# Turning and splitting q and k in the projection stage instead of in attention

## What is computed

```
proj = rmsnorm(x) @ w_in                     # q, k, v (1024 wide each), f, z, xBC, dt, gates
q = rmsnorm(q per head of 64, q_norm_w)      # 16 heads
k = rmsnorm(k per head of 64, k_norm_w)      # is also an output (k_prompt, k_sample)
c = cumsum(log_sigmoid(f + b_f))
s = (q @ k.T) * 64**-0.5 + c[t] - c[s]       # causal; running rows see 256 cached keys too
att = softmax(s) @ v
```

## Time and profile before

| what | value |
|---|---|
| time, median of 3 runs | 2890.07 us (2890.05 to 2894.38) |
| the profiled execution, its own time | 2885.89 us |
| its span, first to last instruction | 2884.1 us |
| mean granted clock of TensorE | 0.978 |
| PE / PEld / DVE / ACT / POOL busy | 95% / 92% / 55% / 35% / 14% |
| DMA queue q1, share of 16 engines | 32.9% |

### The profile page before, as it was taken

One profiled execution on the slowest core, in us unless ns is written; L12 is line 12 of the kernel. 1 busy time (PEld: TensorE's weight loads), 2 busy tenths in 40 slices (PEclk: granted clock), 3 DMA queues, 4 the chain that ended last, 5 costly groups with the idle time before them and its releaser, 6 DMA issues. The chain is left out here.

```text
span 2884.1 us, 47789 instructions
## 1 busy us (share of the span) xinstructions
PE 2737.1 (95%) x18754; PEld 2658.0 (92%) x18754; DVE 1577.2 (55%) x2867; ACT 1022.4 (35%) x2353; POOL 405.7 (14%) x475
## 2 busy tenths in 40 slices
PE   6998979999999999997999989998989999999999
PEld 5997978989999889887999979998989999999999
DVE  4336337656566565565898864464373444434434
ACT  4223336556666655653434331121231111111110
POOL 0000012212122222222555520000000000000000
PEclk8999999999999999998999999999989999999999
DMA  3222232132232222215888873343221111111112
GB/s 115 90 90 53 79 90 91 43 101 76 67 108 76 66 93 58 84 63 140 205 194 214 201 203 121 112 134 128 65 99 58 45 44 45 44 45 44 48 67 96
DMA packets 334448, 273.31 MB, mean 95 GB/s; under 512 B 95952, under 2 KB 311632, under 8 KB 334096
## 3 DMA queue, kind: packets, MB, share of 16 engines
q1 hardware_dynamic: 334224, 270.25, 32.9%
HBM read 197.90 MB, written 72.28 MB: 94 GB/s over the span
## 5 line engine op out<-in xcount | busy, mean ns | idle before, releaser
L411 PE MATMUL banks<-w_hi,xn_hi 128*128 128x256 f32 x1440 | 407.8, 287 | 8.7 <-DVEq L368 5.0
L411 PE MATMUL banks<-w_lo,xn_hi 128*128 128x256 f32 x1440 | 405.5, 286 | 0.0
L414 PE MATMUL banks<-xn_hi,w_hi 128*128 128x352 f32 x1152 | 379.5, 329 | 0.7 <-ACT att_xs L986 0.7
L414 PE MATMUL banks<-xn_hi,w_lo 128*128 128x352 f32 x1152 | 378.7, 329 | 0.0
L414 PE MATMUL banks<-xn_lo,w_hi 128*128 128x352 f32 x1152 | 378.2, 328 | 0.0
L411 PE MATMUL banks<-w_hi,xn_lo 128*128 128x256 f32 x1280 | 366.3, 286 | 0.0
L411 PEld LDWEIGHTS banks<-w_hi,xn_hi 128*128 128x128 f32 x1440 | 276.7, 192 | 10.6 <-DVEq L368 5.1
L411 PEld LDWEIGHTS banks<-w_lo,xn_hi 128*128 128x128 f32 x1440 | 276.6, 192 | 0.2
L1704 PE MATMUL banks<-h_hi,w_hi 128*128 128x352 f32 x768 | 248.8, 324 | 1.9 <-DVEq L1625 1.9
L1704 PE MATMUL banks<-h_lo,w_hi 128*128 128x352 f32 x768 | 248.6, 324 | 0.0
L1704 PE MATMUL banks<-mlp_uhi,w_hi 128*128 128x352 f32 x768 | 248.6, 324 | 0.0
(11 more groups left out here) (293 smaller groups left out, 6160.8 us busy)
## 6 DMA issues: line engine op xcount, KB each, us to landing
w_raw<-in_w_in SPq DMA_DIRECT2D x44, 1024.0 KB, 5.5
scratch_xbc<-att_co SPq DMA_DIRECT2D x32, 512.0 KB, 2.6
ssd_ab<-scratch_acum SPq DMA_DIRECT2D x64, 256.0 KB, 6.0
br_g<-scratch_gates SPq DMA_DIRECT2D x72, 176.0 KB, 2.8
scratch_gates<-hand_tanh SPq DMA_DIRECT2D x48, 176.0 KB, 5.4
scratch_z<-att_z_stage SPq DMA_DIRECT2D x64, 128.0 KB, 1.9
ssd_xbc<-scratch_xbc SPq DMA_DIRECT2D x64, 128.0 KB, 3.4
ssd_xbc<-scratch_xbc SPq DMA_DIRECT2D x128, 64.0 KB, 3.7
```

What stands on the lines that cost most here:

```text
L411: ins = self.nc.tensor.matmul(self.bank(n, P, PW), x[:, k, t * P:(t + 1) * P], w[:, k, :], start=first, stop=end)
L414: ins = self.nc.tensor.matmul(self.bank(n, P, TT), w[:, k, m * P:(m + 1) * P], x[:, k, r * TT:(r + 1) * TT], start=first, stop=end)
```

## The change

The preparation moves from attention to `HeadNormTm`. After a q or k panel is normalized, PE turns it there in blocks of 128 x 128, that is two heads at once, into bank 4; ACT writes the high half (for q with the norm weight and the factor 1/8 as a scale per row), DVE the low half, and SP stores both to two new scratch tensors `q_ops` and `k_ops` [16 heads, 64 + 64 + 4 rows, keys]. There are five groups a panel, one a slot, in slots end + 4 to end + 8, and four groups of cached keys in slots 0 to 3 of the first round. The large reduction is cut into one per tile, in the tile's slot, and the square buffer holds one tile. The weight pass is left for k only. In attention `prep`, `make_hi`, `make_lo` and `double` go; `load_ops` loads each pair as it stands with two DMAs (for keys the first one reads the high rows twice). The freed bank 4 becomes a third bank of the streamed tiles. The bias rows are stored into the same tensors by `Decays`.

```diff
 class HeadNormTm:
+    GROUPS = 5
+    CACHED = 4
+    B_TURNED = 4
...
+    def groups(self, i, n):
+        out = []
+        if i == 0 and 0 <= n < self.CACHED:
+            out.append((n, None))
+        for g in range(self.GROUPS):
+            for k in self.ended(n - 4 - g):
+                out.append((self.CACHED + (i * self.per + k) * self.GROUPS + g, (k, g)))
+        return out
...
     def act(self, act, i, n):
...
             s.nc.scalar.activation(self.stage[x][0:m, t, :], s.bank(n, m, PW), ACT.Copy).then_inc(self.copied, 1)
-            s.nc.scalar.activation(self.sq[0:m, t, :], s.bank(n, m, PW), ACT.Square).then_inc(s.free, 1)
+            if u:
+                act.wait_ge(self.summed, u)
+            s.nc.scalar.activation(self.sq[0:m, :], s.bank(n, m, PW), ACT.Square).then_inc(s.free, 1)
+        for c, src in self.groups(i, n - 1):
+            w = self.width(src)
+            act.wait_ge(self.turned, c + 1)
+            if c >= 2:
+                act.wait_ge(self.ops_stored[c % 2], self.landed(c - 2))
+            s.nc.scalar.activation(self.t_hi[c % 2][:, 0:w], s.core.banks[:, self.B_TURNED, 0:w], ACT.Copy,
+                                   scale=self.scale(src)).then_inc(self.hi_made, 1)
...
     def dve(self, dve, i, n):
...
+        for k, t in s.mine(self, n):
...
+            s.wait_free(dve, i, n)
+            v.tensor_reduce(self.ss[k % 2][0:m, t * self.HEADS:(t + 1) * self.HEADS], self.sq[0:m, :].rearrange("p (h d) -> p h d", d=HD),
+                            AX.X, ALU.add).then_inc(self.summed, 1)
+        for c, src in self.groups(i, n - 1):
+            w = self.width(src)
+            dve.wait_ge(self.hi_made, c + 1)
+            bank, hi, lo = s.core.banks[:, self.B_TURNED, 0:w], self.t_hi[c % 2][:, 0:w].bitcast(F32), self.t_lo[c % 2][:, 0:w]
+            v.scalar_tensor_tensor(out=lo, in0=bank, scalar=self.scale(src), in1=hi, op0=ALU.mult, op1=ALU.subtract).then_inc(self.lo_made, 1)
...
+    def pe(self, pe, i, n):
+        s = self.stream
+        for c, src in self.groups(i, n):
+            if src is None:
+                pe.wait_ge(self.cached, 16)
+            elif src[1] == 0:
+                self.wait_normed(pe, i, src[0])
+            if c:
+                pe.wait_ge(self.lo_made, c)
+            for rows, m, col in self.blocks(c, src):
+                ins = s.nc.tensor.transpose(s.core.banks[:, self.B_TURNED, col:col + m], rows, s.core.ident[0:m, 0:m])
+            ins.then_inc(self.turned, 1)
...
     def sp(self, sp, i, n):
...
+        for c, src in self.groups(i, n - 1):
+            sp.wait_ge(self.lo_made, c + 1)
+            for head, x, cols, col in self.places(i, c, src):
...
+                for part, buf in zip(at, (self.t_hi, self.t_lo)):
+                    sp.dma_start(self.ops[x][head:head + 2, part:part + HD, cols], buf[c % 2][:, col:col + w].bitcast(F32)).then_inc(self.ops_stored[c % 2], 16)
...
 def project_qkv
...
                 for n in range(stream.slots):
                     stream.pe(pe, i, n)
+                    norm.pe(pe, i, n)
...
 def attention_z_xbc
...
-    B_SCORES, B_TURNED, B_PREP, B_OUT, B_TILES = 0, 2, 4, 5, (6, 7)
+    B_SCORES, B_TURNED, B_OUT, B_TILES = 0, 2, 5, (4, 6, 7)
...
-                sp.dma_start(k[:, 0:NT, :], k_prompt[:, cols].rearrange("(t p) d -> p t d", p=P)).then_inc(k_loaded, 16)
...
+            def load_ops(h, g):
...
+                    sp.dma_start(first, q_ops[h, 0:2 * HD, cols]).then_inc(ops_loaded[g], 16)
+                    sp.dma_start(second[0:KX, :], q_ops[h, HD:HD + KX, cols]).then_inc(ops_loaded[g], 16)
...
+                    sp.dma_start(first, k_ops[h:h + 1, 0:HD, cols].to_broadcast([2, HD, cols.stop - cols.start])).then_inc(loaded, 16)
+                    sp.dma_start(second[0:KX, :], k_ops[h, HD:HD + KX, cols]).then_inc(loaded, 16)
...
                 if h + 1 < H:
-                    if u == 0:
-                        load_bias(h + 1, K0)
-                    elif u == 1:
-                        load_bias(h + 1, QA)
-                    elif u == 3:
-                        for g in (K1, QB, KS):
-                            load_bias(h + 1, g)
+                    for g in {0: (K0,), 1: (QA,), 3: (K1, QB), LASTU: (KS,)}.get(u, ()):
+                        load_ops(h + 1, g)
```

More of the change, by code:

```diff
@@ new lines, in places, with width @@
+    def places(self, i, c, src):
+        if src is None:
+            return [(4 * c + 2 * b, 1, slice(TP, TP + PAST), b * PAST) for b in range(2)]
+        k, g = src
+        head = (i * (self.per // 2) + k // 2) * self.HEADS
+        first = 0 if k % 2 == 0 else PAST
+        if g == 4:
+            return [(head + 2 * b, k % 2, slice(TP + first, TP + first + TS), b * TS) for b in range(2)]
+        return [(head + g // 2 * 2, k % 2, slice(g % 2 * 512, (g % 2 + 1) * 512), 0)]
+    def width(self, src):
+        return 2 * TS if src is not None and src[1] == 4 else 512
@@ new lines, in wait_normed @@
+    def wait_normed(self, eng, i, k):
+        if k % 2:
+            eng.wait_ge(self.weighted, (i * self.per + k) // 2 + 1)
+        else:
+            eng.wait_ge(self.scaled, i * self.per + k + 1)
+    def start_sp(self, sp):
+        sp.dma_start(self.w[:], self.weights[1].to_broadcast([P, HD])).then_inc(self.w_loaded, 16)
+        with self.stream.nc.allow_non_contiguous_dma(reason="one value per partition"):
+            for b in range(2):
+                sp.dma_start(self.w_q[b * HD:(b + 1) * HD, :], self.weights[0].rearrange("o (d e) -> d (o e)", e=1)).then_inc(self.w_loaded, 16)
+        rows = self.stage[1][:].rearrange("p t n -> p (t n)")[:, 0:2 * D]
+        sp.dma_start(rows.rearrange("p (t n) -> p t n", t=2), self.cache_k.rearrange("(t p) n -> p t n", p=P)).then_inc(self.cached, 16)
@@ L529, in sp @@
     def sp(self, sp, i, n):
         s = self.stream
[L531 to L536, removed]
+        for k in self.ended(n - 3):
+            if k % 2:
+                self.wait_normed(sp, i, k)
+                cols = bass.ds((i * (self.per // 2) + k // 2) * PW, PW)
+                sp.dma_start(self.to[0][:, cols].rearrange("(t p) d -> p t d", p=P), self.stage[1][:, 0:NT, :]).then_inc(self.stored, 16)
+                sp.dma_start(self.to[1][:, cols], self.stage[1][0:TS, NT, :]).then_inc(self.stored, 16)
@@ L543 @@
+        sp.wait_ge(self.stored, 32 * (self.stream.rounds * self.per // 2))
+        for j in range(2):
+            sp.wait_ge(self.ops_stored[j], self.landed(count - 1 - (count - 1 - j) % 2))
 class Decays:
@@ L1897, in _ @@
             stream.start_sp(sp)
-            load(0)
-            for g in SEQ:
-                load_bias(0, g)
+            load_ops(0, K0)
+            load_ops(0, QA)
+            load_v(0)
+            for g in (K1, QB, KS):
+                load_ops(0, g)
             for n in range(FIRST):
@@ L1904, in _ @@
                 if u == 0 and h + 1 < H:
-                    load(h + 1)
+                    load_v(h + 1)
                 for slot in range(3):
```

303 lines of the change are left out of this document (103 added, 200 removed).

## The result

| | time, median | against the kernel before |
|---|---|---|
| before | 2890.06 us (4 runs) | |
| after | 3110.86 us (3106.59 to 3114.76, 4 runs) | 1.0763, 95% interval 1.0742 to 1.0784 |

The change made the kernel 221 us slower. The forecast was 2915 us, 25 us slower, with a range up to 2952. The sign was right, the size wrong by a factor of nine, and most of the loss came from something that the sum had at nothing.

The account below looks back on a forecast made before the run. TensorE (PE) work and waits were taken to bound both stages. Projection +78 us (17 transposes, 42 waits, 16 clock, 3 start) and attention -53 gave +25: 2915 us on the median's scale, range 2888 to 2952.

Parts of the forecast that it names:

- rival 4: Projection: high halves wait for stores two groups back; 16 k groups wait some 1 us each, 2931 us; chance 0.12.
- "Nothing" for attention's loads: Attention: bigger operand loads, 1.9 MB a head against 0.6, cost nothing, as DMA share is 0.27 and they issue early.
- PE waits for groups there: Projection, q and cached-key slots: PE waits for ACT's late high half and DVE's low half, 19 times 2.2 us, +42.
- projection, PE busy (transposes and clock): Projection: added transposes cost PE +17 us, half speed after waits +16 us.
- attention, PE busy: Attention: 320 preparation transposes go from PE's work, -34 us.
- attention, waits for scaling: Attention: 19 PE waits for scaled probabilities, 26.6 us, shrink by some 0.2 us each, -4 us, bounds 0 and -12.
- attention, waits for exp: Attention: two 4 us waits for exp go, the raw panel's DMA being issued earlier; -8 us, bounds 0 and -13.
- The stretch of the decays' chain: Projection, second round: DVE's 10.7 us lateness moves from the diagonal into group waits; nothing extra, bounds -3 and +6.
- The clock: Projection: half of 19 PE waits are followed by half speed, 1.7 us each, +16 us, bounds 0 and 32.
- rival 2: Projection: half speed after every wait, 16 us more (2931), or over whole tile stretches, 42 more (2957); chance 0.15.
- Rival 3: Attention: 39 us of exp and scaling waits vanish altogether, 33 us less, 2882 us, not slower; chance 0.12.
- rival 5: Projection: ACT-DVE chain hidden, high half coming early; 42 and 16 us fall away, 2857 us; chance 0.03.

Follow-up runs that it names:

- planes: Kernel after, with high and low halves in scratch planes of their own (128-row stores), 64-row attention loads, halves ahead of copy, square and reduction: 2874.4 us, 0.9958 of before.
- stores and loads split: Kernel after, with each 2-by-64-row store and broadcast key load made two 64-row transfers, 68-row loads made 64 and 4: 2931.1 us, 1.0145 of before.
- the repeat: The kernel after with both the stores and attention's loads split, measured once more unchanged: 2932.6 us, 1.0155 of before.

## Why the forecast failed, point by point

**The step that failed is the price of the stores.** The sum has no term for them. Only rival 4 prices them, "if the 256 KB stores land late behind a panel, each of 16 k groups waits some 1 us": 16 us. Its mechanism was right, the high half of group c waiting for the stores of c-2; its price was taken from a transfer of another form. The earlier trace rows show 1 MB in 5.5 us, and that is a load over 128 rows; in the kernel after, a window with one in flight (176 to 178 us) has a share of 0.92. The engines that carry a transfer do not follow from its bytes. Stores of 2 by 64 rows run at 50 GB/s, so a group's pair needs 10.5 us; ScalarE waited 34 times, 202 us in all, where the rival had 16, and 20 of these waits were for stores of q, which it did not have at all. The chance of 0.12 and the range's end at 2952 were wrong for the same reason: none of the rows read from the trace before shows a transfer of this form, and the form stands in the diff.

**"Nothing" for attention's loads** was the same omission a second time: 21 us, 16 of them the broadcast. The DMA share of 0.27 is a mean over 16 engines and does not tell how many of them one transfer uses.

**The change of stages** had no term. It cost 15 us after, 5 with the transfers split, 1.5 with planes: the last store of v stands behind the stores of the operands on SP, and the next stage's loads behind it.

With the forms mended (stores and loads split) the rest of the sum can be read. The kernel is then 42 us slower than the kernel before by the ratio (45 by the medians), against a forecast of 25, and inside its range. The right column is from the profiled execution, the slowest of four; the repeat has +84 for the projection and -45 for attention.

| term | forecast | stores and loads split |
|---|---|---|
| projection stage | +78 | +87 |
| PE waits for groups there | 19 of 2.2 us | 18 of 2.06 to 2.11 us |
| projection, PE busy (transposes and clock) | 17 + 16 | +46, some 22 of it the transposes |
| attention | -53 | -45 |
| attention, PE busy | -34 | -36 |
| attention, waits for scaling | -4 | -9.5 |
| attention, waits for exp | -8 | +3.5 |
| change of stages | 0 | +5 |

**The lockstep waits were right** in place, number and size. Timeline of PE in the kernel with stores and loads split, a row of them and the start of a later one:

```profile
104.38 0.66 PE L628 MATMUL banks<-ident,qkv_norm_stage 128*128 128x128 f32 x4 [2.11 <-DVE qkv_turned_lo L603]
110.03 0.66 PE L628 MATMUL banks<-ident,qkv_norm_stage 128*128 128x128 f32 x4 [2.11 <-DVE qkv_turned_lo L603]
115.67 0.66 PE L628 MATMUL banks<-ident,qkv_norm_stage 128*128 128x128 f32 x4 [2.11 <-DVE qkv_turned_lo L603]
122.80 0.31 PE L628 MATMUL banks<-ident,qkv_norm_stage 32*128 32x32 f32 x2 [2.11 <-DVE qkv_turned_lo L603]
...
412.24 0.66 PE L628 MATMUL banks<-ident,qkv_norm_stage 128*128 128x128 f32 x4 [2.11 <-DVE qkv_turned_lo L603]
419.38 0.66 PE L628 MATMUL banks<-ident,qkv_norm_stage 128*128 128x128 f32 x4 [2.11 <-DVE qkv_turned_lo L603]
```

and the chain of ScalarE and VectorE that ends the one at 115.67, copy, square, high half, low half, which the forecast had put together from the earlier trace rows:

```profile
113.59 0.38 ACT L562 ACTIVATE qkv_norm_stage<-banks 128x256 f32<-128x256 f32 x1 [4.41 <-PE banks L411]
113.87 0.38 ACT L565 ACTIVATE qkv_sq<-banks 128x256 f32<-128x256 f32 x1
114.14 0.69 ACT L571 ACTIVATE qkv_turned_hi<-banks,qkv_norm_wq 128x512 fp32r<-128x512 f32 x1
```

```profile
114.86 0.75 DVE L603 SCALAR_TENSOR_TENSOR qkv_turned_lo<-banks,qkv_norm_wq,qkv_turned_hi 128x512 fp32r<-128x512 f32 x1 [0.16 <-ACT qkv_turned_hi L571]
```

The stretch of the decays' chain also came out as put: its 10.7 us wait at the diagonal is gone and stands in the group waits as 7.38 and 3.23 us.

**The clock** cost more than forecast, but stayed inside the bounds of its term (0 and 32). Windows of the same kernel, two with a row of such waits, two without:

```profile
103.00:126.00 23.00, 15.28 (x101) 14.63 (x102) 4.68 (x8) 4.25 (x10) 0.00 (x0) 0.87 0.52 134
126.00:190.00 64.00, 63.48 (x527) 63.24 (x527) 25.83 (x42) 20.61 (x54) 0.00 (x0) 0.99 0.35 104
...
338.00:405.00 67.00, 67.00 (x540) 64.36 (x539) 30.00 (x69) 24.33 (x59) 0.00 (x0) 1.00 0.43 111
411.00:437.00 26.00, 18.43 (x101) 17.78 (x102) 4.54 (x8) 4.10 (x10) 0.00 (x0) 0.74 0.47 120
```

0.87 and 0.74 with waits of 2.1 us in them, 0.99 and 1.00 between. The timeline gives the price of one: from one such wait to the next 5.65 us pass at full speed (104.38 to 110.03) and 7.14 with half speed behind the wait (412.24 to 419.38), 1.5 us more. Of the 13 such distances of this kernel 9 are long, not half of them.

The share of the transposes in the +46 us follows from the kernel with planes, which has the same transposes and the clock of the kernel before, 0.97. Its projection stage:

```profile
41.00:405.60 364.60, 344.03 (x2750) 338.63 (x2750) 160.06 (x285) 124.92 (x297) 0.00 (x0) 0.97 0.37 115
```

PE is busy 344 us there against 322 before: at most 22 us for the transposes (17 forecast). The other 25 us with stores and loads split (369 against 344) are the same matmuls at half speed, against 16 forecast. That is nearer to the first half of rival 2, every wait followed by half speed, than to the forecast. Its second half, the clock down for whole stretches, did not happen here; in the kernel after, where the waits are 8 to 10 us, the stage's mean is 0.83. That is a consequence of the stores: with them split it is 0.93, with stores and loads split 0.91. The Trainium skill, TensorE: Matmul & The Clock Gate, section "HAM oscillation — how this bites in real kernels", which the forecast set beside its bound of 32, tells of waits of 3 to 5 us. The waits here are 2.1 us, so it does not decide what follows them; the distances above do.

**Attention** gave the transposes' time as worked out; the waits for exp and scaling fell to 32.8 us and not to 27. The two parts of this term missed in opposite directions, and that they nearly cancel is luck. Waits of PE in the kernel with stores and loads split (L2041 is the turn that waits for the scaling, L2026 the scores that wait for exp), which answer to the earlier trace rows:

```profile
PE banks L2041 <- ACT att_pr L2125: 17.1, 15, 3.6
...
PE banks L2026 <- ACT att_pr L2118: 15.7, 6, 3.9
```

The scaling fell from 26.6 to 17.1 us. The waits for exp were to lose the two of 4 us, because w_raw would be issued earlier, and rose from 12.2 to 15.7: w_raw is now late for ScalarE 6 times (18.0 us) and not 3 (9.2). At the two waits followed back (558.91 and 1106.23) SP still issued it behind seven loads, which took 3.9 and 4.5 us to issue, against eight and 5.9 us before. So the second of these waits is shorter, 2.6 us, and the first one is new. How much of that is the larger bytes of the operands was not taken apart. In the repeat the two sums are 19.3 and 14.4 us: the directions hold, the sizes scatter.

Rival 3 (attention's waits vanish, the kernel not slower) needed 78 us from attention; the best version gives 47. That version is faster than the kernel before all the same, because its projection loses 28 us and not 87. It was reached where rival 5 looked, with most of the chain hidden (group waits of 15 us in all and not 47), and not by rival 3; the order of the list speaks against it only as long as nobody changes the list.

## What to carry to other kernels

Read the form of each new transfer before its bytes: one with a slowest dimension of 2 (two heads, a broadcast to two copies) ran here at the share of two of sixteen engines and 46 to 50 GB/s, whatever the mean DMA share leaves free. Take the price of an unseen transfer from a row of the same form or keep the range open up to bytes over that rate. When a buffer waits for its store, compare the time to landing with the time between fills: 10.5 against 3.3 us decided this case. And lay out scratch so that the rows written together are consecutive. From the kernel after to the one with planes it is 236 us: 158 of them came by the form of the stores, 21 by that of the loads, 42 by the reordering of two engines' lists, and 15 when planes took the place of split transfers.

## What the runs showed of the hardware

- Transfers of 2 by 64 rows: share 0.13 to 0.15 of 16 engines, 50 GB/s with 2 KB in a row, 46 with 1 KB, 39 to 40 with 0.5 KB. The same 256 KB as 128 rows landed in 2.1 to 3.5 us.
- Such a transfer also slows others: w_raw (1 MB over 128 rows) took a median of 14.8 us to land beside them, 5.4 with the stores split; attention's weights came late (35 us of ScalarE's waits after, 9 before) by loads that PE itself waited for only once, 2.9 us.
- An issue of such a store held SP for 0.48 us with nothing ahead of it and for up to 5.8 us behind others still draining, so that everything behind it on SP, loads of other tiles too, came late.
- A wait of 2.1 us ahead of each tile was followed by half speed in 9 of 13 cases, at 1.5 us each.
- Splitting 68 rows into 64 and 4 brought 2.5 us, which the scatter does not tell from nothing. By the rule on the slowest dimension that the Trainium skill, DMA: Bandwidth & Descriptors, gives in its section "Why a DMA increments its semaphore by 16 and not by 1", 68 rows get 4 engines; no run here shows what that costs.
